# Fetching the U and the V rows of an expert lookup apart, from two tables, in rings of 8 and 12

## The reference, cut to what matters

```python
g = jax.nn.softmax(best_s, axis=-1)
u = u_tab[expert]
vv = v_tab[expert]
act = jax.nn.gelu(jnp.einsum('nd,nhkd->nhk', xb, u).astype(jnp.float32), approximate=False)
return jnp.einsum('nhk,nhkd->nd', (g * act).astype(xb.dtype), vv)
```

## Time and profile before

| | us |
|---|---|
| three runs | 2259.5, 2260.71, 2263.51 (median 2260.71) |
| the profiled execution | 2262.2, with a span of 2260.4 |
| busy in the span: TensorE, VectorE, ScalarE, GpSimd | 1911.5, 1242.2, 560.0, 743.8 |
| first indirect DMA issued, last one | 829.6, 2228.0 |

### The profile page before, as it was taken

The page is one execution under the profiler, slowest core; times in us unless marked ns, Lnnn a source line. Parts: engine busy times, 40 slices in busy tenths (PEclk is TensorE's granted clock), DMA queues, the critical chain, the costliest instruction groups (busy, mean ns, idle before and its releaser), DMA issues.

```text
span 2260.4 us, 16445 instructions
## 1 busy us (share of the span) xinstructions
PE 1911.5 (85%) x5468; PEld 913.8 (40%) x5468; DVE 1242.2 (55%) x2843; ACT 560.0 (25%) x1228; POOL 743.8 (33%) x595
## 2 busy tenths in 40 slices
PE   4989999999899996999888878777778877777787
PEld 2433456454454594444444333333333333333333
DVE  4186312443752156555555666666766666666654
ACT  1111122555421034222122221212122122222121
POOL 1035433333000001333333444444444444343441
PEclk8979899999899997999989988999888899899988
DMA  8203114002012234899999999999999999999995
GB/s 337 103 14 149 75 75 158 0 29 84 28 42 112 91 117 183 342 350 350 362 381 372 388 420 420 420 420 420 420 420 416 420 420 420 412 417 418 411 403 236
DMA packets 82532, 624.74 MB, mean 276 GB/s; under 512 B 9088, under 2 KB 9104, under 8 KB 10768
## 3 DMA queue, kind: packets, MB, share of 16 engines
q0 software_dynamic: 73728, 536.90, 58.4%
q1 hardware_dynamic: 8560, 86.54, 9.8%
q10 hardware_dynamic: 160, 0.26, 0.1%
HBM read 621.31 MB, written 2.10 MB: 276 GB/s over the span
## 4 chain that ended last, share of the span: by engine, by line
PE 51%; DMA 36%; DVE 5%; issue 4%; ACT 3%; POOL 0%; DVEq 0%; SPq 0%; POOLq 0%; ACTq 0%
DMA sb<-uv_table,sb 36%; PE ps L880 15%; PE ps L598 7%; PE ps L488 6%; PE ps L806 5%; PE ps L490 4%; PE ps L612 3%; PE ps L775 2%; ACT sb L1160 1%; PE ps L548 1%; PE ps L634 1%; PE ps L648 1%; PE ps L470 1%; PE ps L435 1%; DVE sb L1211 1%
## 5 line engine op out<-in xcount | busy, mean ns | idle before, releaser
L880 PE MATMUL ps<-sb 128*128 128x512 f32 x2048 | 1004.6, 648 | 251.7 <-ACT sb L1160 251.5
L1662 POOL DMA_INDIRECT sb<-uv_table,sb x512 | 554.4, 1083 | 1107.2 <-PE ps L880 789.8
L1533 DVE CUSTOM_DVE_ANT_0 sb<-sb 128x1024 f32<-128x1024 f32 x512 | 629.6, 1230 | 491.4 <-DMA sb<-uv_table,sb 491.4
L880 PEld LDWEIGHTS ps<-sb 128*128 128x128 f32 x2048 | 414.3, 207 | 829.9 <-issue 504.3
L1160 ACT ACTIVATE sb<-sb 128x128 f32<-128x128 f32 x512 | 163.5, 390 | 629.0 <-DVE sb L1542 629.0
L598 PE MATMUL ps<-sb 128*128 128x512 f32 x384 | 172.7, 602 | 2.4 <-DVE sb L1408 1.3
L488 PE MATMUL ps<-sb 128*128 128x512 f32 x304 | 139.9, 615 | 0.0
L1613 POOL TENSOR_SCALAR sb<-sb 128x4096 f32<-128x4096 f32 x6 | 63.7, 10612 | 191.4 <-DMA sb<-w_mod 191.4
L806 PE MATMUL ps<-sb 128*128 128x512 f32 (+2 forms) x352 | 115.6, 483 | 0.8 <-issue 0.8
L1152 ACT ACTIVATE sb<-sb 128x4 f32<-128x4 f32 x128 | 26.3, 206 | 341.1 <-DVE sb L1533 341.1
L598 PEld LDWEIGHTS ps<-sb 128*128 128x128 f32 x384 | 71.9, 191 | 92.0 <-issue 87.0
(11 more groups left out here) (225 smaller groups left out, 1650.9 us busy)
## 6 DMA issues: line engine op xcount, KB each, us to landing
sb<-w_mod SPq DMA_DIRECT2D x12, 2048.0 KB, 8.7
sb<-w_proj SPq DMA_DIRECT2D x8, 2048.0 KB, 12.0
sb<-w_merge SPq DMA_DIRECT2D x6, 2304.0 KB, 8.5
sb<-w_pq SPq DMA_DIRECT2D x11, 1152.0 KB, 10.2
sb<-uv_table,sb POOLq DMA_INDIRECT x512, 15.9
sb<-w_merge SPq DMA_DIRECT2D x3, 1536.0 KB, 6.5
sb<-x SPq DMA_DIRECT2D x1, 2048.0 KB, 8.6
sb<-x_turned SPq DMA_DIRECT2D x1, 2048.0 KB, 14.9
```

The lines of the kernel that those rows point to most:

```text
L880: mm = pe.matmul(bank(2 * (t % 2) + f), dgw[n % NDG], row_v(n)[:, T * f:T * (f + 1)], start=(i == 0), stop=(i == PH * PK - 1))
L1533: dve.tensor_tensor_reduce(out=row_u(n), in0=row_u(n), in1=n2_tm[:, u // PH, :], scale=1.0, scalar=0.0, op0=ALU.mult, op1=ALU.add, accum_o ...
L1662: pool.indirect_dma_start(out=ring[PLACE[n]], out_offset=None, in_=uv_table, in_offset=bass.IndirectOffsetOnAxis(ap=experts[u % 4][:, i:i ...
```

## The change

`uv_table` becomes two inputs, `u_table` and `v_table`, rows of 1024 floats each (4 KB). The ring of whole rows and its table go. `u_ring` has 8 places of 4 KB per partition (area "qa"), `v_ring` 12 (area "w"); it is the memory of the ten places before, and the three later ones aren't used. U row n is asked for once dot n - 8 is done, V row n once lookup n - 12 is weighed. GpSimd's loop alternates: the U row of n, then the V row of n - 4 (`BEHIND`); the last four V rows come by themselves. Each place has its own semaphore; the dot waits for U alone, and TensorE gets a wait for V. All bytes, dots, weights and matmuls are the same; there are 1024 indirect DMAs of 512 KB instead of 512 of 1 MB.

```diff
-        ring = [area("qa", 2 * D * i, 2 * D) for i in range(4)] + [area("w", 2 * D * i, 2 * D) for i in range(6)]
-        ring += [area("n", 2 * D * i, 2 * D) for i in range(2)] + [area("cq", 0, 2 * D)]
-        EARLY, LATE_FROM = 10, 140
...
+        u_ring = [area("qa", D * i, D) for i in range(8)]
+        v_ring = [area("w", D * i, D) for i in range(12)]
+        BEHIND = 4
...
                 pe.wait_ge(s["dg_ready"], n + 1)
+                pe.wait_ge(v_in[n % 12], 16 * (n // 12 + 1))
...
-                dve.wait_ge(row_in[PLACE[n]], 16 * (LAP[n] + 1))
+                dve.wait_ge(u_in[n % 8], 16 * (n // 8 + 1))
...
-            for n in range(NL):
+            def fetch_u(n):
                 u, i = divmod(n, PK)
                 if i == 0:
                     pool.wait_ge(s["picked"], u + 1)
-                if BEFORE[n] is not None:
-                    pool.wait_ge(s["weighed"], BEFORE[n] + 1)
...
+                if n >= 8:
+                    pool.wait_ge(s["dot_done"], n - 7)
+                pool.indirect_dma_start(out=row_u(n), out_offset=None, in_=u_table,
+                                        in_offset=bass.IndirectOffsetOnAxis(ap=experts[u % 4][:, i:i + 1], axis=0))\
+                    .then_inc(u_in[n % 8], 16)
+
+            def fetch_v(n):
+                u, i = divmod(n, PK)
+                if n >= 12:
+                    pool.wait_ge(s["weighed"], n - 11)
+                else:
                     pool.wait_ge(s["yo_done"], 2 * TT)
...
+            for n in range(NL + BEHIND):
+                if n < NL:
+                    fetch_u(n)
+                if n >= BEHIND:
+                    fetch_v(n - BEHIND)
```

More of the change, by code:

```diff
@@ L117, in encoder_layer @@
 def encoder_layer(nc, cst, vec, x, x_turned, w_mod, w_proj, w_small, w_alpha, w_merge, w_out, w_pq,
-                  uv_table, out):
+                  u_table, v_table, out):
     with ExitStack() as ctx:
@@ L241, in encoder_layer @@
         acc_tmp = area("w", 6 * 2 * D, D)
-        ring = [area("qa", 2 * D * i, 2 * D) for i in range(4)] + [area("w", 2 * D * i, 2 * D) for i in range(6)]
-        ring += [area("n", 2 * D * i, 2 * D) for i in range(2)] + [area("cq", 0, 2 * D)]
-        EARLY, LATE_FROM = 10, 140
-        def ring_table():
-            place, before, lap, last = [], [], [], {}
-            for n in range(NL):
-                r = n % EARLY if n < LATE_FROM else (n - LATE_FROM + EARLY) % len(ring)
-                place.append(r)
-                before.append(last.get(r))
-                lap.append(0 if r not in last else lap[last[r]] + 1)
-                last[r] = n
-            return place, before, lap
-        PLACE, BEFORE, LAP = ring_table()
+        u_ring = [area("qa", D * i, D) for i in range(8)]
+        v_ring = [area("w", D * i, D) for i in range(12)]
+        BEHIND = 4
         def row_u(n):
-            return ring[PLACE[n]][:, 0:D]
+            return u_ring[n % 8]
         def row_v(n):
-            return ring[PLACE[n]][:, D:2 * D]
+            return v_ring[n % 12]
         def scores_of(u):
@@ L315, in encoder_layer @@
                    zi_ready share_ready w_ready dg_ready weighed gated2 added stored""".split()
-        row_in = [sem(f"row_in{i}") for i in range(len(ring))]
+        u_in = [sem(f"u_in{i}") for i in range(len(u_ring))]
+        v_in = [sem(f"v_in{i}") for i in range(len(v_ring))]
         s = {nm: sem(nm) for nm in names}
@@ L1654, in _ @@
                     pool.wait_ge(s["picked"], u + 1)
-                if BEFORE[n] is not None:
-                    pool.wait_ge(s["weighed"], BEFORE[n] + 1)
-                elif PLACE[n] in range(4, EARLY):
+                if n >= 8:
[8 more added lines that the diff above has]
+                else:
                     pool.wait_ge(s["yo_done"], 2 * TT)
-                elif PLACE[n] >= EARLY:
-                    pool.wait_ge(s["sc_done"], NQ)
-                    pool.wait_ge(s["tm_done"], 4 * TT)
-                pool.indirect_dma_start(out=ring[PLACE[n]], out_offset=None, in_=uv_table,
+                pool.indirect_dma_start(out=row_v(n), out_offset=None, in_=v_table,
                                         in_offset=bass.IndirectOffsetOnAxis(ap=experts[u % 4][:, i:i + 1], axis=0))\
-                    .then_inc(row_in[PLACE[n]], 16)
+                    .then_inc(v_in[n % 12], 16)
+            for n in range(NL + BEHIND):
[3 more added lines that the diff above has]
+                    fetch_v(n - BEHIND)
 def laid_out(inp):
@@ L1703, in laid_out @@
         "w_out": by_tile(d["w_out"][0]), "w_pq": pq,
-        "uv_table": np.concatenate([d["peer_u"][0], d["peer_v"][0]], 1),
+        "u_table": d["peer_u"][0], "v_table": d["peer_v"][0],
     }
```

## The result

The changed kernel takes 2362.4 us, the median of four runs (2355.0 to 2364.4), beside 2261.7 for the kernel before (four runs, 2259.5 to 2263.5): a ratio of 1.044, with a 95% interval from 1.0415 to 1.0465. It is 4.4% slower. I had forecast 2231 us and a range of 2200 to 2322, so both the number and the range missed. One thing stands ahead of all that follows, since most readings turn on it: the same kernel, unchanged, was later timed on three chips, at 2368.2 (two runs), at 2354.1 (four), and, last, at **2230.1 us** (one run). One of eight runs of the kernel before on chip 12 took 4807.4 us, which nothing here explains; it hardly moves the median.

A forecast was written before the change was run, and what follows sets the result against it. It took the ring as the early bound and the DMA engines as the late one. U row 140 landing at 1258, plus 371 late lookups of 2.57 us (953.5), V halves, stores and end gave 2231 us, range 2200 to 2322.

The forecast's parts named there:

- Head: First lookups: GpSimd no longer waits for the first weighing at 894.3 and goes on at 889.6, some 10 us ahead.
- Early stage: Lookups 12 to 140: ring no longer the bound, 2.80 us a lookup instead of 3.02, about 40 us gained.
- Late stage, DMA: Lookups from 140 on: 4 KB pieces take 2.57 us a lookup, the middle of 2.497 and 2.645.
- rival C: Gathers: random 4 KB pieces cost more than those of x, 2.75 us a lookup at 381 GB/s, 2321 us; chance 0.08.
- Late stage, GpSimd: Late lookups: two issues take 2.48 us, 2.77 with mean holds; which engine holds depends on what times the dots.
- (i): Late lookups: with rows queued, GpSimd falls in step at 2.57 us and the backlog keeps itself; 2200 to 2262, chance 0.52.
- State (ii): Late lookups with an empty DMA queue: holding feeds back, period 2.68 to 2.83 us, about 2.77.
- Rival B: Late lookups: GpSimd sets the pace at 2.77 us, 2292 us in all (2247 to 2322); chance 0.28.
- TensorE, tail: TensorE's waits for V rows are free unless its clock falls; after the last V row, weighing 1.9 and end 5.6 us.
- the lower clock: TensorE, rival D: stops for each V lower its clock, 3.4 us a lookup for a quarter of them, 2310 us; chance 0.05.
- The sum: Whole kernel: U row 140 lands at 1258, 371 late lookups add 953.5, V halves, stores and end follow, 2231 us.
- The range: Whole kernel: from 2200, the lower end of (i), to 2322, holding B to its upper end and most other slow cases.

The follow-up runs named there:

- half_rows: The changed kernel with tables of 512 columns, 2 KB pieces, half the bytes, dots and weighings as long as before: 2394.2 us, repeated on chip 2 at 2408.1 us.
- two near kernels: The changed kernel with dots reading normed tokens from PSUM from lookup 128 on, 2232.1 us; the changed kernel with dots over 64 columns, 2231.3 us; both on chip 15.
- extra_every_second: The kernel before with an extra, unused fetch of 128 pieces of 64 bytes at every second lookup: 2274.2 us.
- n2_in_psum_whole_rows: The kernel before (whole rows) with dots reading the normed tokens from PSUM from lookup 128 on: 2258.9 us, ratio 0.9996.
- a third: The changed kernel with dots reading normed tokens from PSUM from lookup 128 on, 2342.0 us on chip 12, beside the unedited changed kernel there at 2354.1 us.

## Why the prediction was wrong, point by point

*Head*: right. U 12 was asked for at 888.4 (forecast 889.6).

*Early stage*: 2.80 us a lookup was taken. U 140 was asked for at 1263.6 in the recorded run, 2.93 a lookup, against 1248 forecast and 1288.7 before; on chip 2 at 1230.3, 2.69 a lookup. The term is 18 us too high where there are no idles, and 16 us too low where there are. TensorE was the bound, as forecast: busy 100 of the 100 us from 900 on, on chip 2.

*Late stage, DMA*: the middle of 2.497 and 2.645 that I took, 2.57, is what 409 GB/s gives, 1.0486 MB / 409 = 2.564, on both chips without idles in the steady part; over the whole late stage, with the stores and its last 112 us at 390, it is 406 GB/s and 2.604 a lookup, 12.5 us more than my term. The estimate from the Trainium skill (DMA: Bandwidth & Descriptors, "Why small descriptors are slow") was 2.53, below what was measured. The recorded run moved 350 to 370 GB/s, which lies outside both my ends and is rival C's number (381 or less) with another cause: the same run moves 410 GB/s from 1560 to 1575 us, 35 GB/s once what was queued has run out (1578 to 1580) and 286 in the ten after. Its median piece takes no longer than chip 2's, so it isn't C, in which every piece costs more.

*Late stage, GpSimd*: two free issues are 2.48, right in all kernels. "GpSimd falls in step at 2.57 by itself, with 0.09 of holding": on chip 2, 343 of 347 V issues start within a dot and are held by 0.11 us, the U issues by 0.00. That is the state I described, to 0.02 us. **The step that failed is "once there is a backlog (i) keeps it".** It took for granted that every step starts when what it waits for is done, and considered only the paces of GpSimd and of the transfers, which differ by less than 0.1 us a lookup. In the recorded run, a backlog was there too (up to 21.8 us from U issue to dot, 10.5 on average, from 890 to 1230 us), and by lookup 128 it was down to 6. What the runs show in its place: semaphores increased 3 to 7 us late, VectorE idle 24 times between 1300 and 2200 us, and behind that 0.29 us of holds and 0.12 of idle GpSimd a lookup, 2.89 instead of 2.57. That a state with so little margin has nothing to rebuild a backlog with after a stop of 4 us is my reading, not shown by a run of its own: without holds the period on chip 12 was still 2.84, with 0.34 of idle GpSimd in their place. I took a rule that holds between two streams for a property of the whole machine.

*State (ii)*: its price was mis-sized. I put L, the time from a U issue to its dot, at 4.25 to 4.55, and the period at 2.68 to 2.83. In the recorded run L was 6.3 (median; the DMA engines weren't empty), and holds were 0.29 us a lookup; with half rows on chip 2, the DMA engines at 0.63, L was 3.7 and V was held by 0.51, which makes 2.48 + 0.51 = 2.99 of the 3.01 measured. The V issue, not the U issue as in my formula, is the one that meets the dot. Rival B was thus at the wrong price at both ends, and still closest in kind to what was recorded: 2322, its upper end, lacks the idles (0.12 x 383 = 46 us).

*TensorE, tail*: free, as forecast. In the recorded run its granted clock was 0.87 from 1300 to 2200 us, on chip 2 it was 0.91; half_rows had 0.87 without idles, so the lower clock goes with a TensorE that waits more. GpSimd's idles do end at weighings, but TensorE had itself stood idle before them (12.95 us at 1580.75) or its increase came late; a lower clock isn't needed. The end took 16.4 us from the last dot, 17.6 in the sum.

*The sum*: 2231 against 2230.1 on chip 2, where each term can be found. That close, it is luck: dot 140 came 12 us ahead of the sum (1245.9 for 1258), and the late stage took 12.5 us more (966.0 for 953.5). The recorded number differs from it by 132 us that no term held. *The range* left them out because every case was built from rows of one undisturbed trace; that all of them share one assumption, that steps start when what they wait for is done, went unpriced.

What is shown and what isn't: that the changed kernel takes 2230 or 2350 to 2370 with nothing changed in it is shown, the first by one run, with three runs of two near kernels beside it. That the two outcomes went with the set of runs is shown too: all kernels of one set that send two full fetches a lookup fall on the same side. That the chip is the reason, and not the hour, I can't tell, since no chip was used twice. That the idles are late increases of semaphores is shown for those whose marks the traces hold (16 of 24 in the recorded run). Why they come late is not. Instruction fetches didn't line up with them: one of the 24 had a packet of the instruction queues in it or in the 2 us before. Whether they need saturated DMA engines was not settled.

One rival was left untested, and the record points at it: the recording itself. Every time here comes from an execution whose core span and clock were recorded, and on the slow side the trace holds 25 to 44% of the landing increases of the kernels with two fetches throughout; on chips 2 and 15 it holds them all, but for 3 of 13104 in extra_every_second, and on chip 11 it also lacks 105 of 9088 in n2_in_psum_whole_rows, which has one fetch and is not slow. Marks are missing wherever increases come late. Whether the same thing causes both, or the recording slows the engines, would take times without recording, and there are none.

## What to carry to other kernels

A change that takes the slack from two engines at once (here GpSimd at 2.59 of 2.59 us and the DMA engines at 1.03) is worth its best case only as long as nothing stops; ask what rebuilds the margin after a stop of a few microseconds, and if nothing does, give the slow state a price and a chance of its own. Fetch in halves only where it shortens a ring that binds, and whole where the transfers bind: that version gained 0.8% on a chip where the full change lost 4.7% (on chip 2 the full change gained 1.5%, one run of each). And compare kernels on one chip, side by side; two of my experiments "proved" a cause that a third, on the same chip as its partner, shrank from 130 us to 12.

## What the runs showed of the hardware

An indirect DMA of 128 rows costs GpSimd 0.94 to 0.95 us and a gap of 0.30, whether its rows have 64 bytes, 2 KB, 4 KB or 8 KB. It is held by a dot with two SBUF operands for what is left of the dot (mean up to 0.55 us for those that meet one), and not at all by the same dot with one operand in PSUM.

Gathers of 4 KB rows moved at 409 GB/s, of 8 KB rows at 420, in steady stretches. With 128 x 64 bytes more at every other lookup the latter moved 414 instead of 417 from 1300 to 2200 us. A 4 KB piece took its engine 0.162 us (median) in a full queue; with half rows, where the queue is often empty, packets of the same size (two 2 KB rows each) had the same median of 0.159 and a mean of 0.229.

One program on Trainium2 took 2230.1 us on one chip (one run) and 2354.1 on another, 5.6% apart, while the kernel before differed by 0.2% among the same chips. On the slow side semaphores that VectorE and TensorE increase are marked up to 7 us and more after the step is done, instead of 0.01 us, and single steps of VectorE and ScalarE start 2 to 11 us after what they wait for. The traces of the slow side lack over half of the landing marks of the kernels with two fetches throughout, and so give no landing times for them, which those of chips 2 and 15 do.
